# Issuing the first stage's conditioning-weight loads from ScalarE and SyncE instead of SyncE alone

## What is computed

```python
def _layer(x, c, lru_conv, lru_h, dn_conv, dn_S, reset_first, p):
    mod = jax.nn.silu(c) @ p['w_ada'] + p['b_ada']
    sh1, sc1, g1, sh2, sc2, g2 = jnp.split(mod, 6, axis=-1)
    h = _rmsnorm(x, p['norm_mix_w']) * (1.0 + sc1[:, None]) + sh1[:, None]
    mix, new_states = _mixer(h, lru_conv, lru_h, dn_conv, dn_S, reset_first, p)
    x = x + g1[:, None] * mix
    h = _rmsnorm(x, p['norm_ffn_w']) * (1.0 + sc2[:, None]) + sh2[:, None]
    x = x + g2[:, None] * _peer(h, p)
    return x, new_states
```

## Time and profile before

| | |
|---|---|
| time, median of 3 runs | 4238.22 us (4232.46 to 4241.97) |
| the profiled execution's own time | 4238.62 us |
| its span, first to last instruction | 4236.7 us |
| busy over the span: PE, DVE, ACT, POOL | 88%, 71%, 34%, 48% |
| first block's stretch of loads, 52 to 286 us: DMA engines' mean busy share | 0.92 |
| bytes moved in it | 346 GB/s |

### The profile page before, as it was taken

The page is one execution under the profiler, slowest core; times in us unless marked ns, Lnnn a source line. Parts: engine busy times, 40 slices in busy tenths (PEclk is TensorE's granted clock), DMA queues, the critical chain, the costliest instruction groups (busy, mean ns, idle before and its releaser), DMA issues. The chain is left out here.

```text
span 4236.7 us, 66528 instructions
## 1 busy us (share of the span) xinstructions
PE 3724.6 (88%) x24474; PEld 3469.5 (82%) x24474; DVE 3013.7 (71%) x4783; ACT 1456.0 (34%) x1876; POOL 2041.3 (48%) x1142
## 2 busy tenths in 40 slices
PE   6877999999998998997679999999998898998987
PEld 3337998898888897997568898899898898888886
DVE  4777655656663214898977777778878888888886
ACT  5664444443442113222332332332332322232222
POOL 2332222222225133334046776777776767776772
PEclk9988999999997898998999999999999999999998
DMA  7971222222224123222589999999999999999994
GB/s 301 345 298 63 85 67 85 85 75 81 78 70 155 54 100 114 74 78 83 176 314 393 401 411 389 415 412 417 414 399 407 410 404 405 410 416 418 407 416 170
DMA packets 256210, 1090.71 MB, mean 257 GB/s; under 512 B 25352, under 2 KB 78856, under 8 KB 176392
## 3 DMA queue, kind: packets, MB, share of 16 engines
q1 hardware_dynamic: 170512, 543.60, 34.4%
q0 software_dynamic: 73728, 536.90, 30.9%
q10 hardware_dynamic: 11776, 7.52, 0.6%
HBM read 1047.54 MB, written 40.40 MB: 257 GB/s over the span
## 5 line engine op out<-in xcount | busy, mean ns | idle before, releaser
L249 POOL TENSOR_TENSOR wlo<-raw,whi 128x1024 fp32r<-128x1024 f32 x551 | 1344.2, 2443 | 1340.0 <-ACT whi L245 1334.1
L245 ACT CAST whi<-raw 128x1024 fp32r<-128x1024 f32 x670 | 698.6, 1049 | 1303.0 <-DMA raw<-in_u 553.9
L2147 PE MATMUL gps<-chi,whi 128*128 128x320 f32 x2048 | 657.7, 321 | 113.9 <-DVE outacc L2276 83.4
L264 PE MATMUL gps<-hi_d,whi 128*128 128x320 f32 x2048 | 653.1, 319 | 89.0 <-DVE wlo L254 62.3
L2147 PE MATMUL gps<-clo,whi 128*128 128x320 f32 x2048 | 646.4, 316 | 0.0
L2147 PE MATMUL gps<-chi,wlo 128*128 128x320 f32 x2048 | 646.0, 315 | 0.0
L264 PE MATMUL gps<-lo_d,whi 128*128 128x320 f32 x2048 | 643.3, 314 | 0.0
L264 PE MATMUL gps<-hi_d,wlo 128*128 128x320 f32 x2048 | 643.3, 314 | 0.0
L2234 DVE SCALAR_TENSOR_TENSOR dps<-ring,coef,dps 128x2048 f32<-128x2048 f32 x252 | 591.9, 2349 | 5.4 <-DMA ring<-in_v_rows,spi 1.0
L2221 DVE CUSTOM_DVE_ANT_0 ring<-ring,dps 128x2048 f32<-128x2048 f32 x256 | 582.4, 2280 | 0.0
L2147 PEld LDWEIGHTS gps<-chi,whi 128*128 128x128 f32 x2048 | 397.4, 194 | 134.5 <-DVE outacc L2276 95.4
(11 more groups left out here) (391 smaller groups left out, 5946.2 us busy)
## 6 DMA issues: line engine op xcount, KB each, us to landing
raw<-in_u SPq DMA_DIRECT2D x256, 512.0 KB, 10.3
raw<-in_v SPq DMA_DIRECT2D x256, 512.0 KB, 8.2
wada<-in_w_ada SPq DMA_DIRECT2D x88, 1024.0 KB, 6.6
raw<-in_w_in SPq DMA_DIRECT2D x96, 512.0 KB, 3.5
gateD<-gst SPq DMA_DIRECT2D x8, 2560.0 KB, 9.9
gate<-gateD SPq DMA_DIRECT2D x32, 640.0 KB, 12.6
raw<-in_w_out SPq DMA_DIRECT2D x32, 512.0 KB, 4.5
raw<-in_w_q SPq DMA_DIRECT2D x32, 512.0 KB, 4.5
```

The source lines that it names most:

```text
L245: act.copy(whi[:, k.slot, :], raw_of(k)).then_inc(W.hi, 1)
L249: pool.tensor_tensor(wlo[:, k.slot, :], raw_of(k), whi[:, k.slot, :].bitcast(F32), ALU.subtract).then_inc(W.lo, 1)
L264: m = pe.matmul(gps[:, bank, 0:DT], w, x[:, kt, :], start=(kt == 0 and n == 0), stop=(kt == KT - 1 and n == 2))
L2147: m = pe.matmul(gps[:, 2 + dt, 0:DT], w[:, slot, cols], x[:, buf, c, :], start=(c == 0 and n == 0), stop=(c == NG - 1 and n == 2))
```

## The change

`load` becomes `load_quarter(eng, g, q)`, with the same wait and the same DMA. SyncE issues quarters 1 and 3 of each group. ScalarE issues quarters 0 and 2: those of group 0 as its first two instructions, those of group g + 1 in between its own roundings of group g, q0 after hi1 and q2 after hi3. The last group's roundings are taken out of ScalarE's loop, since no load follows them.

```diff
+        def load_quarter(eng, g, q):
+
+            if not (isinstance(g, int) and g == 0):
+                eng.wait_ge(*wada_lo_done(g - 1, q))
+            eng.dma_start(wada[:, q], row(a["w_ada"], g * 4 + q)).then_inc(s_wada[q], 16)
+
...
-                def load(g):
-                    for q in range(4):
-                        if not (isinstance(g, int) and g == 0):
-                            sp.wait_ge(*wada_lo_done(g - 1, q))
-                        sp.dma_start(wada[:, q], row(a["w_ada"], g * 4 + q)).then_inc(s_wada[q], 16)
-
-                load(0)
+                load_quarter(sp, 0, 1)
+                load_quarter(sp, 0, 3)
                 with sp.Fori(1, NGA) as g:
-                    load(g)
+                    load_quarter(sp, g, 1)
+                    load_quarter(sp, g, 3)
...
                 ch = Chain(act, W.act_steps, act_total)
+                load_quarter(act, 0, 0)
+                load_quarter(act, 0, 2)
                 act.wait_ge(S.c, 16)
...
-                def wada_rounded(g):
+                def wada_rounded(g, more=True):
                     for q in range(4):
                         act.wait_ge(s_wada[q], g * 16 + 16)
                         if not (isinstance(g, int) and g == 0):
                             act.wait_ge(S.used, g * 4 + (q - 3))
                         act.copy(wada_hi[:, q], wada[:, q]).then_inc(S.hi, 1)
+                        if more and q % 2:
+                            load_quarter(act, g + 1, q - 1)
 
                 wada_rounded(0)
-                with act.Fori(1, NGA) as g:
+                with act.Fori(1, NGA - 1) as g:
                     wada_rounded(g)
+                wada_rounded(NGA - 1, False)
```

## The result

The changed kernel takes 4253.47 us, median of 6 runs (4242.33 to 4257.40); the kernel before, timed beside it, 4234.83 us (4227.77 to 4241.97). The ratio is 1.0038, 95% interval 1.0024 to 1.0053: slower, by 10 to 22 us. That is inside the range given (4229 to 4262), but the forecast, 4242 us and no measurable change, was too good; of the rivals the slower one came nearest in time (4258 us), and its mechanism was not the one at work.

The account below looks back on a forecast made before the run. The first block was taken as bound by a loop of waits on q1 through GpSimd's lo1. Loop -1.0, start +4.5 and ScalarE's issues 0 gave +3.5 us on 4238.62, 4242 us, range 4229 to 4262.

Parts of the forecast that it names:

- the slower one: Rival: in the first block q2's load holds up q1 every round; +19.5 us with the start, 4258 us, chance 0.33.
- The bound: First block: a loop of waits on q1's single buffer through ScalarE's hi1 and GpSimd's lo1, 11.65 us a clean round.
- The start: Kernel's beginning: q0 and q2 of group 0 share the engines with xT, so xT and all behind come 4.5 us later.
- The long rounds, a gain of 8.4 us: First block's loop: q0 no longer ahead of q1 in one queue, so four long rounds go, gaining 8.4 us.
- Sharing, a loss of 0.45 us in every round: First block's loop: q2 on its own queue shares the engines with q1's end, landing q1 0.45 us later a round.
- The third rival, no change in the loop: Late q1 loads come from the engines, not the queue; long rounds stay, only the start costs: 4243 us, chance 0.07.
- ScalarE's issues, counted at 0: First block: 44 load issues on ScalarE, 18 us in all, counted as 0 because ScalarE has idle time and lo3 covers.
- lo3 as its cover: VectorE is at lo3 until 168.3, so a later hi0 makes lo0 only 0.1 to 0.2 us late.
- 0.2 x 20 = 4 us: Price of the late lo0 over the first block's 20 rounds if lo3 did not cover it; counted as 0.
- hi0 near 39 and the squares near 22: Sign of the start's loss: first square near 22 instead of 17.45, hi0 near 39 instead of 34.70.
- no row of 9 us: Sign of sharing in, long rounds out: GpSimd idle some 7.4 us in nearly every round, no row of 9 us.
- The sign of being wrong in kind: In the first block, hi0 starts at 35, or VectorE by a late lo0, not hi1, releases GpSimd.

Follow-up runs that it names:

- cut-off: Kernels stopped behind the first block, writing out 576 columns of the conditioning result; with nothing else changed 310.36 us, with the whole change 323.82 us.
- the plain order: SyncE issues q0 to q3 of each later group in turn, as in the kernel before; its first block with nothing changed takes 310.36 us.
- the late issues on one queue: Kernel before, SyncE issuing the next q0 only after hi1 and q2 after hi3: 4248.87 us, ratio 1.0032; first block alone 318.44 us.
- split loop: Changed kernel with group 0 all on SyncE, loads split from group 1 on: 4242.95 us, ratio 1.0017; first block alone 318.52 us.

## Why the prediction was right or wrong

**The bound: right.** The loop over q1 through GpSimd was the beat of the block. Taking GpSimd out of it, and with it the turns that it took with VectorE, is what made it faster (299.85 against 310.36 us); giving the loads a second queue did not.

**The start: right in place and size.** +4.5 us were forecast, and hi0 of group 0 starts 4.3 us later. ScalarE's timeline after, beside the earlier trace rows, and the DMA issue of `xT` after and before (KB, us to landing):

```profile
21.64 1.26 ACT L391 ACTIVATE sq<-xT 128x576 f32<-128x576 f32 x2 [10.25 <-DMA xT<-in_x_t]
...
39.02 3.68 ACT L398 CAST wada_hi<-wada 128x2048 fp32r<-128x2048 f32 x2
...
xT<-in_x_t SPq DMA_DIRECT2D x1, 4608.0 KB, 19.5
```

```profile
xT<-in_x_t SPq DMA_DIRECT2D x1, 4608.0 KB, 15.3
```

`xT` lands 4.2 us later, and everything behind it moves. In the first block alone it is worth 3.4 us, by medians of runs that overlap; the whole kernel's runs can't resolve it.

**The long rounds, a gain of 8.4 us: wrong.** The step that failed is "q0 no longer stands ahead of q1 in one queue". With q0 on a queue of its own and nothing else moved, the time stayed at 310.73 us and late q1 loads were still there. That they come with a q0 that is still landing was seen, and the count by q0's landing bears it out; that the queue makes them was only inferred.

**Sharing, a loss of 0.45 us in every round: not seen.** Clean rounds after have the same 7.00 us of idle time as before, and q0 on a second queue costs nothing that can be seen. The q1 loads that are not late land after a median of 4.8 us with q2 on ScalarE as without, where 5.1 to 5.2 was forecast. The slower rival rested on this mechanism, q1 held up every round, and so was right in time and wrong in cause: what grew is mostly the number of long rounds. In the cut-off profiles seven or eight of 20 rounds are over 12.4 us with q2 on ScalarE, one or two with the plain order or q0 alone, and five with the late issues on one queue. The whole kernels' profiles differ less: five and four with q2 on ScalarE, four and two with the plain order, five with the late issues.

**The third rival, no change in the loop: half right.** For a queue as such it holds: with q0 on the second queue or nothing the block takes 310.7 or 310.4 us. The Trainium skill's page "DMA: Bandwidth & Descriptors", section "Issuing engines are not separate DMA queues", says that issuing from several engines only saves issue time, and these two times agree. The rival left out what the issuing engine itself loses.

**ScalarE's issues, counted at 0: this is the step that decided.** The place was named, the wait for lo2 ahead of hi0, with lo3 as its cover. The size was wrong twice. First, hi0 was put at 0.5 us later than before, and it is 1.0 later: 0.8 us pass from the start of the issue to hi0, not the 0.4 of the issue's own row. The rest is the end of ScalarE's loop. q2's issue is the last instruction of its body, so the jump back (line 403) now stands between a wait that ends late and hi0:

```profile
L403 ACTq ALU_OP  x1: 41/41/41, 62.3 to 62.3; - x1
L403 ACTq COMPARE_BRANCH  x1: 50/50/50, 62.4 to 62.4; - x1
L403 ACTq FUSED_REGOPS  x1: 50/50/50, 62.6 to 62.6; - x1
```

Ahead of the loop, with no jump behind the issue, the next rounding starts 0.37 us after the issue's start:

```profile
43.26 0.33 ACTq L348 DMA_DIRECT2D wada<-in_w_ada  x1
43.63 3.70 ACT L398 CAST wada_hi<-wada 128x2048 fp32r<-128x2048 f32 x2 [0.93 <-DVE wada_lo L368]
```

Second, the price "0.2 x 20 = 4 us" counted only VectorE's delay in the round. The late lo0 also delays the load of the next q0 by 0.7 us, and that load is still landing when the next q1 is issued. That more long rounds follow from this later q0 is what the count by q0's landing and the late issues on one queue speak for. The count also leaves q2's bytes beside the end of q1 no visible part in it. A kernel that issues q2 from ScalarE without holding up hi0 would be the direct test; it was not run.

**Its own criteria.** hi0 near 39 and the squares near 22 came true; "no row of 9 us" did not. The four rows of over 9 us are the sign that had been set for the third rival, to which the least chance was given. The sign of being wrong in kind, a late lo0 that releases GpSimd, was close: hi1 still releases it in every row, but a late lo0 works on it by way of the next q0.

What stays open: 10.3 of the 18.8 us between the two profiles are in the first block, and the cut-off kernels put 13.5 there; the rest is within the spread of runs and was not traced. Why single q1 loads take 7 us instead of 4.7, in every variant with lo1 on GpSimd, was not found either. The landings narrow it down: a load counts as landed with the last of its 16 parts, and in 27 of the 49 late ones 15 parts had landed within 5.2 us; in one of the changed kernel 15 had after 4.77 us and the last after 7.49.

## What to carry to other kernels

A load that is issued from an engine that also computes stands in that engine's order: its wait and its issue delay the instruction behind it, together with a loop's jump where the issue is the last of the body, and the price is what that instruction releases, not the issue's own length. Before giving a stream of loads a second queue, look which wait closes the loop; here it was a slow subtraction on GpSimd, and moving that to VectorE gave 10.5 us where the split loop lost 8 and the whole change 13. Where one execution differs from the next by more than the effect, cut the program off behind the block in question and time that.

## What was not expected

- On ScalarE hi0 starts 0.76 to 0.80 us after the start of q2's issue (169.89 to 170.65, 61.93 to 62.73), though the issue's row shows 0.34 to 0.35 us: the loop's jump back stands between them. Without it the difference was 0.37 us.
- Two loads ahead of everything else on the second queue delayed not only `xT` but the small constants: `ct`, 72 KB, takes 9.0 us to land instead of 3.8.
- The number of long rounds varies between executions of the same block: four in the profile of the whole kernel before, one in that of its first block alone.
